# Feed-forward steps of a two-block transformer kernel: VectorE's list in another order, the first sum multiplied before the next form, and the gated units turned behind the first conventional piece

## The reference

```
ffn = (silu(h2 @ w_gate) * (h2 @ w_up)) @ w_down     # block 1; x = x + gt2 * ffn
h   = h + (silu(y @ w_gate_2) * (y @ w_up_2)) @ w_down_2     # block 2
```

## Time and profile before

| what | value |
|---|---|
| median of 3 runs | 2300.13 us (2298.36 to 2301.72) |
| the profiled execution's own time | 2300.74 us |
| its span | 2299.0 us |
| TensorE busy, VectorE busy, ScalarE busy | 97%, 84%, 59% of the span |
| granted TensorE clock, mean | 0.994 |

### The profile page before, as it was taken

The page is one execution under the profiler, slowest core; times in us unless marked ns, Lnnn a source line. Parts: engine busy times, 40 slices in busy tenths (PEclk is TensorE's granted clock), DMA queues, the critical chain, the costliest instruction groups (busy, mean ns, idle before and its releaser), DMA issues.

```text
span 2299.0 us, 30974 instructions
## 1 busy us (share of the span) xinstructions
PE 2226.5 (97%) x10284; PEld 1769.0 (77%) x10284; DVE 1936.1 (84%) x2190; ACT 1364.2 (59%) x1688; POOL 91.3 (4%) x125
## 2 busy tenths in 40 slices
PE   6899999999999999999999999999999999999998
PEld 3577757787888888888878887877888888888786
DVE  4376878989999999999975998599999999999765
ACT  3233367465676766666655444557666676667654
POOL 1101030000000000000011000000000000000020
PEclk9999999999999999999999999999999999999999
DMA  9999995866666666666646565675666666666554
GB/s 389 396 364 358 412 357 205 321 225 195 201 193 200 193 200 198 198 198 201 209 146 211 174 185 167 188 239 191 195 199 200 200 201 207 194 202 192 182 182 148
DMA packets 131567, 518.23 MB, mean 225 GB/s; under 512 B 14497, under 2 KB 20257, under 8 KB 118305
## 3 DMA queue, kind: packets, MB, share of 16 engines
q1 hardware_dynamic: 121552, 449.11, 59.3%
q0 software_dynamic: 9216, 67.11, 7.2%
q10 hardware_dynamic: 720, 0.99, 0.1%
HBM read 512.96 MB, written 4.19 MB: 225 GB/s over the span
## 4 chain that ended last, share of the span: by engine, by line
PE 52%; DVE 19%; issue 8%; ACT 3%; DVEq 1%; DMA 0%; ACTq 0%
PE ps L2499 31%; PE ps L2677 18%; DVE sum_w_lo L1697 5%; DVE sum_raw L1715 2%; DVE sum_raw L1736 2%; ACT w_hi_more L984 2%; DVE w_lo L1973 2%; DVE raw L1721 1%; DVE w_lo L1690 1%; DVE raw_more L1721 1%; PE ps L2641 1%; PE ps L2487 1%; DVE gate L2242 1%; PE ps L2962 0%; ACT w_hi L984 0%
## 5 line engine op out<-in xcount | busy, mean ns | idle before, releaser
L984 ACT ACTIVATE w_hi<-raw 128x1024 fp32r<-128x1024 f32 (+1 forms) x432 | 447.8, 1048 | 336.7 <-PE ps L2677 252.6
L1973 DVE TENSOR_TENSOR w_lo<-raw,w_hi 128x1024 fp32r<-128x1024 f32 (+1 forms) x242 | 292.6, 1218 | 151.7 <-ACT w_hi L984 147.1
L2677 PE MATMUL ps<-w_hi,fm_hi 128*128 128x512 f32 (+1 forms) x840 | 333.3, 397 | 4.0 <-DVE w_lo L1973 2.6
L2677 PE MATMUL ps<-w_lo,fm_hi 128*128 128x512 f32 (+1 forms) x864 | 336.1, 389 | 0.0
L864 ACT ACTIVATE sum_w_hi<-sum_raw 128x1024 fp32r<-128x1024 f32 x180 | 189.6, 1054 | 206.2 <-DVE sum_raw L1715 148.8
L2677 PE MATMUL ps<-w_hi,fm_lo 128*128 128x512 f32 (+1 forms) x776 | 301.7, 389 | 0.0
L1697 DVE TENSOR_TENSOR sum_w_lo<-sum_raw,sum_w_hi 128x1024 fp32r<-128x1024 f32 x180 | 219.5, 1219 | 16.0 <-ACT sum_w_hi L864 13.8
L984 ACT ACTIVATE w_hi_more<-raw 128x1024 fp32r<-128x1024 f32 x198 | 202.0, 1049 | 34.8 <-DVE raw L1721 27.0
L1690 DVE TENSOR_TENSOR w_lo<-raw,w_hi 128x1024 fp32r<-128x1024 f32 x180 | 216.2, 1219 | 7.4
L1690 DVE TENSOR_TENSOR w_lo<-raw,w_hi_more 128x1024 fp32r<-128x1024 f32 x180 | 216.3, 1220 | 6.9
L2677 PEld LDWEIGHTS ps<-w_hi,fm_hi 128*128 128x128 f32 x840 | 159.3, 190 | 61.0 <-issue 26.1
(11 more groups left out here) (399 smaller groups left out, 4624.7 us busy)
## 6 DMA issues: line engine op xcount, KB each, us to landing
raw<-in_w_up SPq DMA_DIRECT2D x152, 512.0 KB, 3.6
raw<-in_w_down SPq DMA_DIRECT2D x132, 512.0 KB, 4.1
ada_raw<-in_w_ada POOLq DMA_DIRECT2D x64, 1024.0 KB, 10.8
raw<-in_w_in SPq DMA_DIRECT2D x120, 512.0 KB, 4.0
raw<-in_w_gate SPq DMA_DIRECT2D x112, 512.0 KB, 3.7
raw<-in_w_out SPq DMA_DIRECT2D x64, 512.0 KB, 3.6
raw_more<-in_w_gate SPq DMA_DIRECT2D x64, 512.0 KB, 3.6
raw_more<-in_w_down SPq DMA_DIRECT2D x44, 512.0 KB, 3.5
```

The lines of the kernel that those rows point to most:

```text
L984: act.activation(hi_tile(like)[:, :, 0:width], raw_tile(like)[:, :, 0:width], ACT.Copy).then_inc(hi_ready, 1)
L1973: dve.tensor_tensor(lo_tile(p)[:, :, 0:width], raw_tile(p)[:, :, 0:width], hi_tile(p)[:, :, 0:width], ALU.subtract).then_inc(lo_dve, 1)
L2677: last = pe.matmul(banks[t][:, 0:width], a, b, start=kt == 0 and k == 0, stop=kt == kts - 1 and k == 2)
```

## The change

PE takes the form u0 before v0, and turns the gated units behind c0 in place of behind b11. ACT makes w0's high part at the end of the list ahead of a step, before `sums_out` 3, and the down pieces' high parts earlier. DVE's list becomes: sum_u0, hidden_next, low b11, sum_v0, low c0, sum_w0, low v0, low u0, low b22, sum_z0; then low b21, low w0, hidden_lo; then for k = 1 and 2 a `group`. Ahead of the first step `hidden_first` stands in front of low b11. In the last step PE turns after three down parts, and ACT and DVE take the last pieces p and p+1 sooner. The operations on PE, ACT, DVE and SP stay the same in kind and number.

```diff
-STEP_ORDER = (("b11", 0), ("c", 0), ("v", 0), ("b22", 0), ("u", 0), ("b21", 0), ("w", 0), ("c", 1), ("z", 0),
+STEP_ORDER = (("b11", 0), ("c", 0), ("u", 0), ("v", 0), ("b22", 0), ("b21", 0), ("w", 0), ("c", 1), ("z", 0),
...
-TURN_AFTER = ("b11", 0)
+TURN_AFTER = ("c", 0)
...
                 hidden_hi(i + done + 1)
-                sum_hi(i, "w", 0)
                 piece_hi(i, "c", 1)
                 sum_hi(i, "z", 0)
...
-                down_hi(i, 2, 3, 4)
+                down_hi(i, 2, 3, 4, 5)
                 sums_in(i, 1)
-                down_hi(i, 5)
+                down_hi(i, 6)
                 sums_out(i, 0)
                 sums_in(i, 2)
+                down_hi(i, 7)
                 step_silu(i)
-                down_hi(i, 6, 7)
                 sums_out(i, 1)
                 sums_in(i, 3)
...
                 early_his(i + 1, 0)
                 sums_out(i, 2)
+                sum_hi(i + 1, "u", 0)
                 early_his(i + 1, 1)
-                sum_hi(i + 1, "u", 0)
                 piece_hi(i + 1, "b21", 0)
+                sum_hi(i + 1, "w", 0)
                 sums_out(i, 3)
...
             down_his(i)
+            p = a + 24 * (FFN_STEPS - 1)
+            splits(p, p + 2)
+            sums_out(i, 2)
             hidden_hi(i + done + 2, last_hi)
-            sums_out(i, 2)
-            p = a + 24 * (FFN_STEPS - 1)
-            splits(p, p + 1)
+            splits(p + 2, p + AHEAD)
             sums_out(i, 3)
-            splits(p + 1, p + AHEAD)
...
-            def early(i, between=None):
+            def early(i):
-                sum_u(i, 0)
                 piece_low(i, "b11", 0)
+                sum_v(i, 0)
                 piece_low(i, "c", 0)
-                sum_v(i, 0)
-                if between:
-                    between()
                 sum_w(i, 0)
                 piece_low(i, "v", 0)
+                sum_low(i, "u", 0)
                 piece_low(i, "b22", 0)
+                sum_z(i, 0)
+
+            def group(i, k):
+
+                sum_low(i, "z", k - 1)
+                sum_u(i, k)
+                piece_low(i, "c", k)
+                sum_v(i, k)
+                piece_low(i, "b11", k)
+                sum_w(i, k)
+                piece_low(i, "v", k)
+                piece_low(i, "b22", k)
+                sum_z(i, k)
+                sum_low(i, "u", k)
 
             def middle(i):
-                sum_low(i, "u", 0)
-                sum_z(i, 0)
                 piece_low(i, "b21", 0)
                 sum_low(i, "w", 0)
                 hidden_lo(i + done + 1)
...
+                group(i, 1)
                 piece_low(i, "b21", 1)
                 sum_low(i, "w", 1)
...
+                group(i, 2)
+                piece_low(i, "b21", 2)
                 sum_low(i, "w", 2)
-                piece_low(i, "b21", 2)
                 sum_low(i, "z", 2)
                 piece_low(i, "c", 3)
...
             def step_body(i):
 
                 middle(i)
+                sum_u(i + 1, 0)
+                hidden_next(i)
                 early(i + 1)
...
                 last_pieces = a + 24 * (FFN_STEPS - 1)
+                hidden_next(i)
+                rests(last_pieces, last_pieces + 1)
+                if not done:
+                    settle(0)
+                rests(last_pieces + 1, last_pieces + 2)
                 hidden_lo(i + done + 2, last_hi, last_lo)
                 if not done:
-                    settle(0)
-                rests(last_pieces, last_pieces + 1)
-                rests(last_pieces + 1, last_pieces + (2 if done else 3))
-                if not done:
                     settle(1)
-                    rests(last_pieces + 3, last_pieces + 4)
                     settle(2)
-                    rests(last_pieces + 4, last_pieces + 5)
+                    rests(last_pieces + 2, last_pieces + 5)
...
-            early(0, hidden_first)
+            sum_u(0, 0)
+            hidden_first()
+            early(0)
...
-            down(i, range(0, 2))
+            down(i, range(0, 3))
             pe.wait_ge(gate_read, i + done + 2)
             turn_hidden(i + done + 2)
-            down(i, range(2, 4))
+            down(i, range(3, 4))
```

More of the change, by code:

```diff
@@ L950, in act_ffn @@
             early_his(0, 0)
+            sum_hi(0, "u", 0)
             early_his(0, 1)
-            sum_hi(0, "u", 0)
             piece_hi(0, "b21", 0)
+            sum_hi(0, "w", 0)
             with act.Fori(0, FFN_STEPS - 2) as i:
@@ L1719, in sum_v @@
                 b12, b22 = at_piece("v", k), at_piece("b22", k)
+                summed(i, "u", k)
                 landed(i, b22)
@@ L1800, in middle @@
                 down_lows(i, (4, 5, 6, 7))
-                hidden_next(i)
             def step_body(i):
                 middle(i)
+                sum_u(i + 1, 0)
+                hidden_next(i)
                 early(i + 1)
```

## The result

The changed kernel takes **2311.36 us** (median of 5 runs, 2309.96 to 2311.81) beside 2300.29 us for the one before (2298.36 to 2302.51): 1.0048 times, 95% interval 1.0035 to 1.0061. It is 11.1 us slower; 12.9 were forecast. The profiled execution has its own time of 2311.73 us and a span of 2310.0 us.

A forecast was written before the change was run, and what follows sets the result against it. TensorE was taken to bound the step, with VectorE close behind. Steady steps +17.6, first steps +6.9 and ends -11.6 sum to +12.9 us, giving 2313.0 us, range 2298 to 2324.

The forecast's parts named there:

- The head of the list: VectorE's list start in each step: later transposes delay hidden_hi and z0, holding VectorE 0.75 us before low z0.
- The stretch to low w2: VectorE from sum_u1 to low w2: 22 places, 25.03 us, so low w2 starts at 1019.71.
- six holds: VectorE between sum_u1 and low w2: six places waiting on the operation in front or ACT, 1.13 us together, expected to go.
- rival C: VectorE's holds of 0.2 us stay with their operations: +2.1 us a step, about 2335 us; chance 0.05.
- The holds on PE: PE's waits in a steady step: 1.52 us at c2, none at v2, another 0.81 at w2.
- The term of 17.6 us: Steady steps: PE's w2 starts 0.98 us later in each of 18, +17.6 us.
- The first steps: First step of each part: hidden_first ahead of three operations makes PE 3.44 us later, twice, +6.9 us.
- The ends: End of each part: PE's waits go, -7.6 us in block 1 and -4.0 in block 2, together -11.6 us.
- Moved at no cost: ACT's down pieces, next step's sum_u, SP's loads and other moved operations: no cost; VectorE's 1.31 us stand goes.
- A: VectorE not held at low z0: a step gains 0.22 us, not 0.98; 2299.4 us, no change; chance 0.10.
- B: Head does not bind, both PE waits close: -1.35 us a step, 2271 us; chance 0.09, including other ways.

The follow-up runs named there:

- single-part run: Kernel before with only the transposes moved behind c0: 2340.82 us, 1.0177 times the kernel before.
- ScalarE swap: Changed kernel with z0's high part ahead of c1's on ScalarE: 2298.03 us, 0.9989 times the kernel before.
- e8_woven_again: Changed kernel with transposes behind b11 again, first step's start as before, low c2 ahead of low z1, low w2 ahead of low b21: 2267.96 us.
- e1_turn_b11: Changed kernel with the transposes behind b11 again, all else of the change kept: 2292.19 us, 0.9966 times the kernel before.

## Why the prediction was right

**The head of the list.** Forecast: hidden_hi 1.08 us behind the transposes, z0 ready 2.95 us behind hidden_hi's start. Rows: 1.07 and 2.96 (997.27 - 996.20, 1000.23 - 997.27). The hold before z0 is 0.76 us start to start, where 0.75 was worked out the same way. The single-part run shows the cause, the ScalarE swap the share of z0.

**The stretch to low w2.** 22 places of 1.1375 us make 25.03 us; the trace has 24.98. So the six holds of the earlier trace rows's kind do go when another operation stands between, and rival C with them. Their reason was put loosely: in most of these pairs the second operation does not need the first one's result. It writes over a piece or a sum that the first has just read (low b11 behind sum_u1), and waits for its signal; low v waits for ScalarE. The Trainium skill ("VectorE: DVE Perf Modes", section "The DRAIN you can't avoid") has a semaphore between two Vector operations cost nothing extra. The traces differ: 1.35 us from sum_u to the low part right behind it before, and 1.14 us a place with a stranger between (sum_u1, low c1, sum_v1 and low b11 in the changed kernel: 1001.37, 1002.50, 1003.64, 1004.77).

**The holds on PE.** 1.52 at c2 and 0.81 at w2 were forecast, 1.47 and 0.78 are there, none at v2. A step of the loop is 0.92 us longer, 0.98 were forecast. The term of 17.6 us measured 17.7 over the nine steps of each part, and that close a match is partly luck: the last step grew by 1.53 and 1.50 us. The forecast took it for a step like the others, but before it was 0.5 us shorter. Of that, 0.37 us is on the stretch from sum_u1 to low w2 (1121.25 to 1144.76, 23.51 us and not 23.88), where the same neighbours stand 1.25 us apart and not 1.34 (sum_z2 at 1143.51 to low w2 at 1144.76). Why they stand closer outside the loop stays open.

**The first steps.** 3.44 forecast, 3.38 and 3.37 measured. PE's stand in front of b11 is 2.87 us in its row (2.6 forecast), and the clock does fall behind it: the weight loads lie 0.43 us apart, where 0.227 is usual, and the granted clock over 539 to 543 us is 0.57, so that most of this stretch ran at the level of 1.2 GHz. These loads are in front of waits for VectorE and cost nothing, as the prediction had it:

```profile
539.36 0.25 PEld L2496 LDWEIGHTS ps<-w_hi_more,fm_hi 128*128 128x128 f32 x1 [2.87 <-DVE w_lo L1691]
...
540.34 0.33 PEld L2496 LDWEIGHTS ps<-w_hi_more,fm_hi 128*128 128x128 f32 x1
540.77 0.33 PEld L2496 LDWEIGHTS ps<-w_hi_more,fm_lo 128*128 128x128 f32 x1
```

**The ends.** -11.6 forecast, -11.3 measured, with the slow clock of the earlier trace rows in it. The split was off: the wait for the last units is removed by the transposes' move, and most of it also by the steady step's lists (low b21 ahead of low w2, ScalarE's down pieces sooner), and I gave all of it to the first.

**Moved at no cost.** The stand for a down piece went from 1.31 to 0.47 us and not to nothing. And sum_u of the next step, which the prediction had some 1 us behind VectorE's arrival, waits 2.04 us for its load:

```profile
1046.56 1.22 DVE L1716 TENSOR_TENSOR sum_raw<-raw 128x1024 f32<-128x1024 f32 x1 [2.04 <-DMA raw<-in_w_up]
```

It is VectorE's longest wait in a steady step (18.0 us over nine). It costs nothing here, as VectorE still arrives 1.38 us too early at hidden_lo, whose time comes from PE's transposes.

**The rivals.** A needed z0 behind hidden_lo at once; it is what the ScalarE swap makes, and its 2299.4 is near that run's 2298.0. B was priced wrongly, though its chance was rightly small: with the head free, VectorE does not close PE's waits, since it is then held by the buffers of w and z. Its 1.35 us a step measured 0.11 (63.11 against 63.22; 0.17 without the last step). That hold was in the code of before (`place_free`) but not in its profile at these sums, and I had read only sum_u's. The error left in the total is mostly the 2.2 us of the unchanged stretch at the front of the profiled run.

## What to carry to other kernels

When a list is rewoven, find the one wait in it that hangs on another engine's progress and count places from there to the last hold of the bound engine: saved gaps ahead of that wait are worth nothing, and each place behind it moves the last hold by a whole place (15 places from 999.73 to 1016.77 above). What the step pays or wins of it is less when another hold then ends last: one place less, with low c2 sooner, gave 0.8 us a step. Moving a producer later (here transposes by 2.7 us, which alone cost 2.3 us a step) costs whatever its consumers' lists can't reorder around; check each in-order list it passes through, here ScalarE's and then VectorE's. And before pricing "the waits close", look in the code for the buffers that are written once per round: they are the next wait, and no profile shows them while the writer is late.

## What the runs showed of the hardware

- An operation of VectorE that waits for the signal of its direct neighbour starts 0.1 to 0.2 us later than one that does not: sum_v behind sum_u 1.25 us (1000.11 to 1001.36 in e8_woven_again), low b11 behind sum_u 1.35 us, unheld operations 1.14 us. In the last step of the kernel before, which stands outside the loop, low b11 follows sum_u at 1.26 us (1121.25 to 1122.51).
- VectorE's sum into a buffer that PE has just used starts 0.20 us after the start of PE's next matmul behind the last use. In e1_turn_b11 the last matmul that uses z0 starts at 999.30, the next at 999.53 and sum_z1 at 999.73; in e8_woven_again these are 992.87, 993.09 and 993.29. From the last use's start it is 0.43 and 0.42 us.
- In the changed kernel the stand before 539.36 (2.87 us in its row, 2.83 us above the usual spacing of the loads) was followed by a granted clock of 0.57 over 539 to 543 us, partly the level of 1.2 GHz. In the kernel before, PE's matmul at 2162.43 starts 3.14 us after the one in front of it (2159.29), 2.91 us above the usual spacing, and the granted clock over 2163 to 2166 us was 1.00. So of these two stands the longer one was not followed by the lower level: the length of the stand alone doesn't decide.
